# Two transformer blocks on one core: identity products in TensorE's waits, and the recurrence's inverse joined to 128 rows

## The reference

```python
def first_block(x, ...):
    z = _rms_norm(x, norm_mix_pre) @ w_in_first
    q, k, v = z[..., :512], z[..., 512:1024], z[..., 1024:1536]
    zs = _token_shift(z[..., 1536:], mu_shift)
    attn = _rms_norm(_dilated_attention(q, k, v), attn_out_gain)   # 8 heads of 64
    rw = _rwkv7(r_r, k_r, v_r, xw, xa, xg, ...)                    # 8 heads of 64
    x = x + _rms_norm(concatenate([attn, rw]) @ w_out, norm_mix_post)
    f = square(relu(_rms_norm(x, norm_ffn_pre) @ w_ffn_up)) @ w_ffn_down   # 4096
    return x + _rms_norm(f, norm_ffn_post)

def step(state, inp):                      # the recurrence in _rwkv7, over the tokens
    sa = einsum('bhij,bhj->bhi', state, kk_t)
    state = state * w_t - sa * b_t + v_t * k_t
    y = einsum('bhij,bhj->bhi', state, r_t)

def second_block(x, mem, ...):
    proj = rmsnorm(x) @ w_in
    merged = sigmoid(gate_c) * conformer_conv(u_glu) + sigmoid(gate_a) * (fox_attention(...) @ w)
    x = x + merged @ w_out
    x = x + cross_attention(rmsnorm(x), rmsnorm(mem), ...)
    x = x + hierarchical_moe(rmsnorm(x), ...)    # 16 experts of 256, 4 groups, 2 experts a token
    return rmsnorm(x, norm_final_g)
```

## Time and profile before

| | us |
|---|---|
| median of 3 runs | 1574.36 |
| lowest, highest | 1573.97, 1576.19 |
| the profiled execution | 1576.64 |
| its span in the trace | 1574.4 |

### The profile page before, as it was taken

One profiled execution on the slowest core, in us unless ns is written; L12 is line 12 of the kernel. 1 busy time (PEld: TensorE's weight loads), 2 busy tenths in 40 slices (PEclk: granted clock), 3 DMA queues, 4 the chain that ended last, 5 costly groups with the idle time before them and its releaser, 6 DMA issues.

```text
span 1574.4 us, 19313 instructions
## 1 busy us (share of the span) xinstructions
PE 1473.1 (94%) x7736; PEld 1154.6 (73%) x7736; DVE 739.1 (47%) x1156; ACT 604.9 (38%) x948; POOL 464.0 (29%) x162
## 2 busy tenths in 40 slices
PE   6999997899879999999998999999999988699995
PEld 5878876688668888888876887666687867577762
DVE  3356277733353532515132596334352335566663
ACT  4443245322353332323134124533333444255552
POOL 2352122000225664646423444320134520200002
PEclk9999998657899999999998999999999999799998
DMA  6232112000135445354432333200123521889964
GB/s 209 87 121 68 56 66 95 2 1 1 46 129 160 135 146 159 124 158 142 139 107 80 98 112 99 80 27 27 49 85 107 188 58 67 346 314 422 419 261 188
DMA packets 97803, 203.90 MB, mean 130 GB/s; under 512 B 6672, under 2 KB 56208, under 8 KB 91056
## 3 DMA queue, kind: packets, MB, share of 16 engines
q1 hardware_dynamic: 90656, 176.94, 32.6%
q10 hardware_dynamic: 4752, 17.30, 2.7%
q0 software_dynamic: 2304, 8.39, 1.4%
HBM read 168.54 MB, written 34.08 MB: 129 GB/s over the span
## 4 chain that ended last, share of the span: by engine, by line
PE 83%; DVE 6%; ACT 5%; issue 3%; DMA 2%; POOL 1%; SPq 0%; POOLq 0%; DVEq 0%; ACTq 0%
PE bank L517 21%; PE bank L499 12%; PE bank L501 12%; PE bank L500 12%; PE bank L2770 4%; PE bank L780 3%; PE bank L799 3%; PE bank L790 2%; PE bank L1193 2%; PE bank L782 1%; ACT whi L428 1%; PE bank L706 1%; PE bank L2716 1%; PE bank L1149 1%; PE bank L1252 1%
## 5 line engine op out<-in xcount | busy, mean ns | idle before, releaser
L436 POOL TENSOR_TENSOR wlo<-raw,whi 128x2048 fp32r<-128x2048 f32 (+2 forms) x83 | 378.7, 4562 | 698.1 <-ACT whi L428 672.0
L428 ACT ACTIVATE whi<-raw 128x2048 fp32r<-128x2048 f32 (+1 forms) x84 | 159.1, 1894 | 279.6 <-PE bank L501 272.1
L517 PE MATMUL bank<-alo,whi 128*128 128x512 f32 x368 | 149.5, 406 | 4.9 <-DVE alo L728 4.9
L1986 DVE TENSOR_TENSOR ffn_relu<-ffn_relu 128x512 f32<-128x512 f32 x32 | 97.7, 3052 | 107.0 <-ACT ffn_relu L1966 107.0
L517 PE MATMUL bank<-ahi,whi 128*128 128x512 f32 x368 | 146.5, 398 | 0.0
L499 PE MATMUL bank<-alo,whi 128*128 128x512 f32 (+1 forms) x360 | 141.1, 392 | 0.0
L501 PE MATMUL bank<-ahi,wlo 128*128 128x512 f32 (+1 forms) x360 | 140.3, 390 | 0.0
L500 PE MATMUL bank<-ahi,whi 128*128 128x512 f32 (+1 forms) x360 | 140.1, 389 | 0.0
L517 PE MATMUL bank<-ahi,wlo 128*128 128x512 f32 x368 | 91.7, 391 | 0.0
L517 PEld LDWEIGHTS bank<-alo,whi 128*128 128x128 f32 x368 | 71.3, 194 | 23.5 <-DVE alo L728 6.1
L517 PEld LDWEIGHTS bank<-ahi,whi 128*128 128x128 f32 x368 | 71.4, 194 | 15.5 <-issue 0.7
(11 more groups left out here) (483 smaller groups left out, 3005.2 us busy)
## 6 DMA issues: line engine op xcount, KB each, us to landing
raw<-in_w_in_dram SPq DMA_DIRECT2D x18, 1024.0 KB, 5.1
expert_gate_up<-in_expert_w_gate_dram SPq DMA_DIRECT2D x17, 1024.0 KB, 11.8
expert_gate_up<-in_expert_w_up_dram SPq DMA_DIRECT2D x17, 1024.0 KB, 14.2
expert_down<-in_expert_w_down_dram SPq DMA_DIRECT2D x17, 1024.0 KB, 9.2
raw<-in_w_ffn_up_dram SPq DMA_DIRECT2D x16, 1024.0 KB, 6.2
raw<-in_w_ffn_down_dram SPq DMA_DIRECT2D x16, 1024.0 KB, 5.6
raw<-in_w_in_first_dram SPq DMA_DIRECT2D x12, 1024.0 KB, 5.5
expert_rows_dram<-zero_rows SPq DMA_DIRECT2D x23, 512.0 KB, 6.9
```

The source lines that it names most:

```text
L428: nc.scalar.activation(whi[:, n % SPLIT, 0:k * c], raw[:, n % RAW, 0:k * c], ACT.Copy).then_inc(hi_made, 1)
L436: nc.gpsimd.tensor_tensor(wlo[:, n % SPLIT, 0:k * c], raw[:, n % RAW, 0:k * c], whi[:, n % SPLIT, 0:k * c].bitcast(F32), ALU.subtract).the ...
L517: ins = nc.tensor.matmul(acc, of, by, start=first and i == 0, stop=last and i == products - 1)
L1986: nc.vector.tensor_tensor(relu2[:, n % 2, :], relu[:, n % 2, :], relu[:, n % 2, :], ALU.mult).then_inc(up_sq, 1)
```

## The change

Four parts.

**Identity products.** `keep_busy(acc, n)` multiplies the identity by the identity, 512 columns in float32, n times, into a bank that is overwritten afterwards. They are placed ahead of waits: 5, 2, 1, 2 ahead of mix1's tiles and 3 behind the last; 3 ahead of the attention's t0, 2 each ahead of t7 to t10, 5 ahead of cross of pair 2; 14 ahead of tile 3 of the ffn turn and 4 behind; 8 and 5 ahead of tiles 2 and 3 of mix2 and 3 behind; 6 ahead of the ranks and 8 ahead of tile 0's picks. 77 in all.

**The inverse joined to 128 rows.** x gives the transposed block directly; `x_rows` gives the same block by rows, `t64` its product with the unit's lower left 64x64 block, `x64` the lower left part of the 128-row inverse; then one product w of 128x128x128 a unit makes all right sides. `w0`, `r`, `w1` and DVE's `rest` are gone. POOL zeroes six upper blocks instead of two. The number of stages is unchanged.

**Preparation of pairs 2 and 3.** POOL multiplies aaa by e_inv (`ae`) instead of kk by aaa and makes r behind DVE's kappa; of rv1, the second half stands behind the norm products; DVE's shift of it stands in pair 3's stage; the copies to high and low parts of pairs 0 and 1 and the w_out slab on POOL come after the preparation.

**The last expert tile.** Tile 16 (`KEPT`) is neither stored nor gathered: its y stays in SBUF, and PE multiplies it by `kept_w`, a matrix of weights that picks its rows (8 small products from 8 DVE operations in the routing). The gathers wait for tiles 14 and 15 only; the down product of tile 15 stands ahead of the last gate-up half; the tiles of rows are summed in the order 0, 1, 3, 2, and tile 3's left half on DVE.

```diff
+        def keep_busy(acc, n):
+
+            for _ in range(n):
+                to = acc[:, :].rearrange("p (a n) -> p a n", n=P)
+                nc.tensor.matmul(to, ident, ident.unsqueeze(1).broadcast_to([P, to.shape[1], P]), start=True, stop=True, skip_group_check=True)
...
             for t in range(st["tiles"]):
+                if t in busy:
+                    keep_busy(banks.open(pe, f"{name}/{t}.0"), busy[t])
...
+                if then and t == st["tiles"] - 1:
+                    keep_busy(banks.open(pe, then[0]), then[1])
...
+                    acc = banks.open(pe, f"{name}/t{j}")
+                    keep_busy(acc, busy.get(j, 0))
                     pe.wait_ge(probs_made, base + j + 1)
-                    acc = banks.open(pe, f"{name}/t{j}")
...
-        FILL_LAST = [0, 6, 6, 0, 3, 1, 1, 1, 1, 1, 1] + [1] * INVERT_PARTS + [2, 2, 2, 2, 2, 2, 2, 2, 2, 3, 3, 3, 3, 2, 2]
+        FILL_LAST = [0, 6, 3, 0, 3, 4, 1, 1, 1, 1, 1] + [1] * INVERT_PARTS + [2, 2, 2, 2, 2, 2, 2, 2, 2, 3, 3, 3, 3, 2, 2]
...
-            in_turn(pe_turn(pe, "mix1", normal1_of))
+            in_turn(pe_turn(pe, "mix1", normal1_of, busy={0: 5, 1: 2, 2: 1, 3: 2}, then=("lora0/0", 3)))
...
+            if p == 2:
+                keep_busy(acc, 5)
             pe.wait_ge(*batch_at("dve", p, "inv"))
...
+            acc = banks.open(pe, u + "x_rows")
+            second = slice(BLOCK, 2 * BLOCK)
+            for n in range(8):
+                ins = nc.tensor.matmul(acc[second, n * BLOCK:(n + 1) * BLOCK], b.inverse_t[second, n, second], b.minus_t[second, n, :],
+                                       start=True, stop=True)
...
+            for n in range(8):
+                nc.tensor.matmul(acc[bottom, n * HD:n * HD + BLOCK], b.ab[top, 0, n, bottom], b.minus_t[top, n, :], start=True, stop=True)
+                ins = nc.tensor.matmul(acc[bottom, n * HD + BLOCK:(n + 1) * HD], b.ab[second, 0, n, bottom], inv[second, m0 + n, :],
+                                       start=True, stop=True)
...
+                ins = nc.tensor.matmul(acc[top, n * HD:(n + 1) * HD], b.minus_t64[bottom, n, :], b.inverse_t[bottom, n, bottom],
+                                       start=True, stop=True)
...
             for i in range(2):
-                acc = banks.open(pe, f"{u}w0{i}")
+                acc = banks.open(pe, f"{u}w{i}")
                 for c in range(NCH):
-                    ins = nc.tensor.matmul(acc[top, c * P:(c + 1) * P], inv64_t[top, m0 + 4 * i + c, :], b.kb[top, i, c, :], start=True, stop=True)
-                banks.filled(ins, f"{u}w0{i}")
...
+                    ins = nc.tensor.matmul(acc[:, c * P:(c + 1) * P], b.inverse_t[:, 4 * i + c, :], b.kb[:, i, c, :], start=True, stop=True)
+                banks.filled(ins, f"{u}w{i}")
...
+            if p == 3:
+                dve_shift(dve, 13)
             st.after("act", "e_inv")
             st.done(tt(b.khat[:, :], b.kmod, b.e_inv, ALU.mult), "khat")
-            st.after("pool", "ka")
-            st.done(tt(b.beta[:, :], b.ka, b.e_inv, ALU.mult), "beta")
+            st.after("pool", "ae")
             st.after("dve", "kk")
+            st.done(tt(b.beta[:, :], b.kk, b.ae, ALU.mult), "beta")
...
-            st.after("dve", "kk")
-            st.done(tt(b.ka, b.kk, b.aaa, ALU.mult), "ka")
+            st.after("act", "e_inv")
+            st.done(tt(b.ae, b.aaa, b.e_inv, ALU.mult), "ae")
+            st.after("dve", "kappa")
             st.after("act", "e_in")
...
+                upper = [(slice(HD, 2 * HD), slice(0, HD)), (slice(BLOCK, HD), slice(0, BLOCK)), (slice(HD + BLOCK, 2 * HD), slice(HD, HD + BLOCK))]
+                for i, (of, (rows, columns)) in enumerate(itertools.product(pairs, upper)):
+                    nc.gpsimd.memset(of.inverse_t[rows, :, columns], 0.0).then_inc(batch_done["pool"], 1)
...
-            pe_rows_close(pe, ["out.0.1", "out.1.1"], ["mix.0", "mix.1"], pe_turn(pe, "ffn", normal2_of))
+            pe_rows_close(pe, ["out.0.1", "out.1.1"], ["mix.0", "mix.1"], pe_turn(pe, "ffn", normal2_of, busy={3: 14}, then=("up.0.0/0", 4)))
...
-                                  pe_turn(pe, "mix2", normal3_of), acts=acts)
+                                  pe_turn(pe, "mix2", normal3_of, busy={2: 8, 3: 5}, then=("glu_gate0/0", 3)), acts=acts)
...
+            acc = banks.open(pe, "ranks")
+            keep_busy(acc, 6)
             pe.wait_ge(picks_made, 3)
-            acc = banks.open(pe, "ranks")
...
+            keep_busy(TURN_BANKS[0], 8)
             pick_rows(pe)
             pe_first_gate_up(pe)
+            turn_kept_picks(pe)
...
-            for i in range(SURE - 2, SURE):
-                tile_done(pool, y_stored, i, 16)
+            for i in range(KEPT - 2, KEPT):
+                pool.wait_ge(*y_stored_at(i))
```

391 lines of the change are left out of this document (229 added, 162 removed).

## The result

| | us |
|---|---|
| before, median of 4 runs | 1574.26 |
| changed, median of 4 runs (1585.31 to 1590.26) | 1587.17 |
| ratio, 95% interval | 1.0081 (1.0068 to 1.0094) |
| span of the profiled execution, changed | 1584.5 |

Intervals are 95% intervals, and ratios of the experiments are to the kernel before on the same chip, over executions within 1.5% of their kernel's fastest, which leaves out two of the four of the last experiment.

The account below looks back on a forecast made before the run. It took TensorE as the limit, at half clock from 298.3 to 371.0 us, with waiting time and lost clock to win. Terms summed to -27.1 us off the median 1574.36: 1547 us, range 1530 to 1563.

Parts of the forecast that it names:

- The inverse of pairs 0 and 1: Joined stages of pairs 0 and 1 take 7.0 us for 9.9, with 0.9 given back: -2.0 us (-4 to +1).
- t64 1.0 (as many records as t): In the inverse of pairs 0 and 1, the new t64 products take 1.0 us, sized by t's record count.
- The stretch of pairs 2 and 3: From 298 to 375 us, cross to q and g: q at 354.3 for 371.0, q and g 2.1 shorter, -18.8 us.
- The clock holds through cross and merge and then falls: Pairs 2 and 3: full clock from cross at 301.0 through merge, then half from about 310, PE waiting for DVE.
- w lifts the clock midway: Pairs 2 and 3: w's 7.0 us of unbroken 128-row products, from 346.0, raise the clock; q at 354.3 us.
- Rival (a): The clock holds from 298 us on; q at 337.5 for 371.0, -35 for -18.8: 1531 us, chance 0.20.
- the attention beside the inversion: Identity products ahead of t7 to t10 and cross, 11.1 us, move cross from 298.25 to about 301.0: +2.7 us (0 to +4).
- The preparation: Pairs 2 and 3: reordered work fills the 7.85 us wait at full clock, masks at 247.7: -9.4 us (-12 to -4).
- if little waits: Condition in pairs 2 and 3's preparation: PE's own 19.9 us from 227.8 puts the masks at 247.7.
- The tail: Kernel's end: gathers no longer wait for the last tile's store, end near 1569 for 1571.4: -2.4 us (-5 to +1).
- (e): Rival: identity products lift no clock and run at 1.71 us wherever it fell: 1626 us, chance 0.05.
- The rule of the Trainium skill: Transposes don't count as busy for the clock; preparation of pairs 2 and 3 gives -5 for -9.4: 1552 us, chance 0.05.

Follow-up runs that it names:

- the last experiment: Changed kernel with t64 in two loops, fitted identity-product counts and products ahead of merge, t, x, t64 and x64: 1552.56 to 1591.43 us in four runs, ratio 0.9919.

## Why the prediction was wrong, point by point

**The inverse of pairs 0 and 1** (forecast -2.0, measured +11.3) is the term that turned the sign. The failing step is "t64 1.0 (as many records as t)". The count was right, the price wrong twice over: t's records use 32x32 tiles that move over the array, 0.02 us a record, while t64's lie on tiles of 64x64 and 32x64 that stay, 0.066 a record (4.2 us), and in turns of 64 and 32 rows, 0.114 and, with the clock falling, 0.15 (9.7 us). I took the row nearest in count, not in shape, and gave no upper bound for it, though w0's records of the same 64x64 tile, 0.107 us, stood beside it. With it came 3.6 us for x64 and the first half of w at half clock, and 1.7 for the merge, which stalled there too. The change's own theory that one product of 128 rows is cheaper than three stages of 64 held for w alone, 3.8 us for 9.9 at full clock; the stages that it needs eat all of it.

**The stretch of pairs 2 and 3** (forecast -19.4 up to q, measured -3.3; the 2.1 behind it came, -2.0). "The clock holds through cross and merge and then falls" was right in place: it fell near 315, behind the merge, which ended at 314.6. "w lifts the clock midway" was right: it rose at 369.5, in w, which began at 366.7. What failed is the sizes: t64 took 11.2 us for 1.9, and the merge's stage 5.6 us more than written, 1.8 by the stall, 2.7 by its items, mostly at half clock, 0.7 by a longer wait for DVE. The cause of the fall was not what I wrote (a wait for DVE) but first the stall, which ended 1.0 us ahead of it, while that wait began 5.4 us behind it. The wait for DVE isn't cleared by that: where the stall was taken away from the joined inverse, the clock fell in it (311.8). The three products that held the clock were tried with the old inverse, which has no such wait.

**Rival (a)**, the clock holding to q, got 0.20 and 1531. The changed kernel didn't do it, but it could be had: 1538.6 to 1539.5 with the old inverse, and holding it is worth 27 us there (1566.8 to 1539.5). I should have asked what a held clock needs; the merge, 192 records in 2.3 us at full clock in pairs 0 and 1, was in the trace.

**Identity products.** The price, 0.857 us, was right to a hundredth: 28 records in 12.29 us with the last one's tail. PE's timeline, which answers to the earlier trace rows:

```profile
464.08 12.29 PE L699 MATMUL bank<-consts 128*128 128x512 f32 x28
476.20 1.04 PE L715 MATMUL bank<-consts,normal 128*128 128x128 f32 x8
477.08 3.60 PE L699 MATMUL bank<-consts 128*128 128x512 f32 x8
480.11 0.80 PE L518 MATMUL bank<-alo,whi 128*128 128x512 f32 x1
```

ffn (+3.2 for +4.3), mix2 (+0.8 for +1.5), routing (+1.0), start (-1.7 for -1.3) and the attention beside the inversion (+2.8 for +2.7) came out as reckoned, +6.1 together for +8.2. They were to be paid back by the clock in the stretch, and weren't. Alone, on the kernel before, the products cost 9.6: the prediction had no term for what they do to a merge far behind them, 4.6 us there.

**The preparation** (forecast -9.4, measured -5.0, and 6.5 to 7.5 by itself). The step that failed is "if little waits". DVE's shift of rv1's second half now stands ahead of pair 3's khat and waits until ACT has evacuated that product:

```profile
246.52 0.75 DVE L1542 SCALAR_TENSOR_TENSOR zv<-bank,cols,zv 128x511 f32<-128x511 f32 x1 [2.51 <-ACT zv L1370]
```

and the three identity products there began in a falling clock, 5.1 us for 2.6. beta took 0.68 us, as foreseen, in both pairs. (A slip in the reading of before: two of DVE's other five products were as long as the first beta, khat of pair 2 took 1.34.)

**The tail** (-1.8 here, -3.4 to -3.8 alone, for -2.4) and the **routing** were right. The first gather came at 1553.83, not at 1542.6, since all stood 12 us later.

**Not in the forecast at all:** the 4.8 us in the forget attention. All 17 traces have the same instructions there and a wait of 1.47 to 1.57 us; the clock fell in five, the changed kernel and four of the experiments. All five have identity products in the turns, as has one of the twelve in which it held. So it goes with these products, though the nearest stand some 170 us ahead; by what, no run shows.

**The chances.** Slower had 0.05, by a mechanism (e) that was wrong in itself: identity products do lift the clock. The range's upper end was 24 us short. What it lacked was an upper bound for the new products' own price. With t64 and x64 at what they took in both halves the sum comes out some 20 us higher, near 1567: the stalls, the clock behind them and the preparation's wait make up the rest.

The rule of the Trainium skill ("TensorE: Matmul & The Clock Gate", Part 4: PE-mode transpose), by which transposes would hold no clock, decided nothing: the term it would have changed came out at -5.0, its number, but for another reason, the wait on DVE; the transposes from 258.8 to 260.6 ran at full clock, 0.11 us each, 1.9 us after the clock had risen in the last of the three identity products. Nor are the ten rows a clean case against the rule: the eleventh, in their midst, is a score product of 2.07 us.

## What to carry to other kernels

Before small products are rearranged, price them by a row of their own tile and neighbours, not by their count: the same number of records took 1.1, 4.2 or 9.7 us here. Sort them by tile; going from one to the other at each product doubled their cost. When the clock falls in a long stretch, look for the one place where it is lost: here three fillers of 0.86 us there were worth 28 us (1566.8 to 1538.6), while the change's 77, none of them there, cost 10. Where PE stands with no releaser amid very short products, look for an instruction packet in the DMA view, and put a longer product ahead. Count fillers by their price against the wait they fill, and then look at the dense stages behind them, however far: they may stall where they didn't.

## What the runs showed of the hardware

- Records of 32 columns in float32, at full clock: 0.02 us each in 32x32 tiles that move over the array (t), 0.032 on one 32x32 tile (x_rows), 0.06 to 0.066 on one tile of 32x64 or 64x64 (t64 sorted), 0.114 when the tile changes between 64 and 32 rows at each product. How the last three differ in cause was not taken apart further.
- PE stalls that fit used-up instructions: 17 stalls of 0.57 to 2.57 us, 15 of them among 192 to 224 records of 16 columns or 128 of 32 in a row and 2 right behind such, ended 1.2 to 1.5 us after a 16 KB packet of the instruction queue q8. Twelve fell in a merge at full clock, five in or behind cross or merge at half clock. Products of 0.86 us between the records took the stall away, in every kernel that had them.
- Whether such a stage stalls depends on where the packets fall: the same 192 records at full clock stalled in three kernels and not in eight.
- In pairs 0 and 1 the clock fell in or right behind the merge in all 8 kernels whose merge stalled, and in none of the 9 whose merge didn't.
- The granted clock may fall or hold in the same code behind the same wait (1.47 to 1.57 us: fell in 5 of 17 kernels), and one kernel that loses the clock in one of its runs took 1552.56 to 1591.43 us in four.
